# Fourteen products of the identity on TensorE behind the last turn of a decoder's front

## The reference, cut to what matters

```
h = rmsnorm(x, lp['ln_mix_g'])      # x (tokens, 2048)
proj = h @ lp['w_in']               # w_in (2048, 4352)
```

## Time and profile before

| what | us |
| --- | --- |
| runs of the kernel before, median | 2083.53 |
| the three runs | 2083.18, 2083.53, 2086.49 |
| the profiled execution | 2078.16 |
| its span, first to last instruction | 2076.5 |
| end of TensorE's last turn in `load_front` | 30.07 |
| first product of `project_in` | 36.12 |

### The profile page before, as it was taken

One profiled execution on the slowest core, in us unless ns is written; L12 is line 12 of the kernel. 1 busy time (PEld: TensorE's weight loads), 2 busy tenths in 40 slices (PEclk: granted clock), 3 DMA queues, 4 the chain that ended last, 5 costly groups with the idle time before them and its releaser, 6 DMA issues. The chain is left out here.

```text
span 2076.5 us, 38289 instructions
## 1 busy us (share of the span) xinstructions
PE 1879.5 (91%) x15850; PEld 1277.5 (62%) x15850; DVE 706.3 (34%) x1361; ACT 511.4 (25%) x866; POOL 140.1 (7%) x180
## 2 busy tenths in 40 slices
PE   6999996788989989989878999999999999999993
PEld 6999985675665549978544555444554444455441
DVE  4447767425545544355441111111111111111111
ACT  4446532232213222263241101110111011101111
POOL 0000000400132300000000000000000000000000
PEclk9999996788999999999988999999999999999997
DMA  8545521113133429443869999999999999999996
GB/s 227 143 124 140 142 74 23 24 39 101 62 112 111 136 78 287 120 142 94 318 253 375 423 422 424 423 426 395 410 422 425 422 423 401 412 424 422 422 424 223
DMA packets 210765, 543.62 MB, mean 262 GB/s; under 512 B 44536, under 2 KB 168538, under 8 KB 183632
## 3 DMA queue, kind: packets, MB, share of 16 engines
q1 hardware_dynamic: 202274, 532.97, 67.3%
q0 software_dynamic: 7936, 8.68, 2.0%
q10 hardware_dynamic: 438, 0.32, 0.1%
HBM read 524.86 MB, written 28.59 MB: 267 GB/s over the span
## 5 line engine op out<-in xcount | busy, mean ns | idle before, releaser
L2848 PE MATMUL p_u<-w_expert,xgT 128*64 128x256 f32 x2048 | 239.6, 388 | 34.0 <-DMA w_expert<-in_w_up_dram 34.0
L2848 PE MATMUL p_g<-w_expert,xgT 128*64 128x256 f32 x2048 | 231.9, 379 | 0.9 <-DVE xgT L2928 0.9
L2848 PEld LDWEIGHTS p_u<-w_expert,xgT 128*64 128x64 f32 x2048 | 148.6, 140 | 117.6 <-DMA w_expert<-in_w_up_dram 43.1
L2864 PE MATMUL p_y<-w_expert,hidT 128*64 128x512 f32 x960 | 217.8, 595 | 0.8 <-DVE hidT L2940 0.5
L2848 PEld LDWEIGHTS p_g<-w_expert,xgT 128*64 128x64 f32 x2048 | 147.1, 137 | 88.0 <-issue 18.8
L2816 PE MATMUL p_xg<-low,slot_sel 128*64 128x512 f32 x768 | 179.7, 604 | 5.2 <-DVE slot_sel L2912 5.2
L2864 PEld LDWEIGHTS p_y<-w_expert,hidT 128*64 128x64 f32 x960 | 66.2, 137 | 126.0 <-issue 124.1
L2933 DVE CAST row<-rowf 128x1 int32<-128x1 f32 x32 | 4.9, 154 | 357.6 <-POOLq L3023 357.6
L2983 ACT ACTIVATE act_g<-p_g 128x256 f32<-128x256 f32 x32 | 12.3, 384 | 429.2 <-PE p_u L2848 429.2
L3020 POOL DMA_INDIRECT x_dram<-y_slots,row x32 | 49.9, 1559 | 973.2 <-DVE y_slots L2944 973.2
L2816 PEld LDWEIGHTS p_xg<-low,slot_sel 128*64 128x64 f32 x768 | 52.9, 138 | 86.0 <-issue 75.6
(11 more groups left out here) (571 smaller groups left out, 2614.4 us busy)
## 6 DMA issues: line engine op xcount, KB each, us to landing
w_expert<-in_w_gate_dram SPq DMA_DIRECT2D x64, 2048.0 KB, 22.6
w_expert<-in_w_up_dram SPq DMA_DIRECT2D x64, 2048.0 KB, 24.7
w_expert<-in_w_down_dram SPq DMA_DIRECT2D x60, 2048.0 KB, 20.3
w_in_raw<-in_w_in_dram SPq DMA_DIRECT2D x32, 1024.0 KB, 5.6
lat<-in_cache_kv_latent_dram SPq DMA_DIRECT2D x128, 128.0 KB, 2.1
ho_raw<-in_w_out_dram SPq DMA_DIRECT2D x12, 1024.0 KB, 6.7
tables_sb<-in_w_out_dram SPq DMA_DIRECT2D x4, 1024.0 KB, 8.3
mem_k_s<-in_cache_mem_k_dram SPq DMA_DIRECT2D x8, 512.0 KB, 6.6
```

The source lines that it names most:

```text
L2848: mm = pe.matmul(acc[SL * h:SL * h + SL, 0:FF // 2], xgT[:, t, g // 2, :], w[g][:, FF * t + FF // 2 * h:FF * t + FF // 2 * h + FF // 2], s ...
L2864: mm = pe.matmul(p_y[SL * h:SL * h + SL, 512 * b:512 * b + 512], hidT[:, j, g, :], tile, start=(g == 0 and j == 0), stop=(g == 1 and j == 1))
```

## The change

Behind the last turn, TensorE waits until ScalarE has made its ninth copy, that of bank `p_r[0]` for the third token tile, and then multiplies the identity by the identity fourteen times into the first 128 columns of that bank. Each is a product of its own (it starts and stops its sum). Nobody reads the result.

```
                 turn_raw(2)
                 turn_scaled(1)
                 turn_scaled(2)
+                pe.wait_ge(raw_copied, 9)
+                for _ in range(14):
+                    pe.matmul(p_r[0][:, 0:128], S.ident, S.ident, start=True, stop=True)
```

## The result

| | median, us | runs |
| --- | --- | --- |
| before | 2083.67 | 22, from 2077.05 to 2090.59 |
| changed | 2089.55 | 22, from 2084.91 to 2095.24 |

The ratio is 1.0025, with a 95% interval of 1.0016 to 1.0035: the change makes the kernel slower by 5.9 us, where no change (2083.6, range 2080.5 to 2087) was forecast.

What follows compares the result with a forecast made beforehand. TensorE was busy 91% of the span, with front shifts carried on. Barrier +0.7 us, partly offset by a warmer clock, left -0.1 to +0.4 us; +0.1 on the 2083.53 median gave 2083.6 us, range 2080.5 to 2087.

Steps and rivals of the forecast that it cites:

- What bounds the kernel, and the meeting of the blocks: Front's end: barrier opens 0.28 us after VectorE, the last to arrive; a front shift reaches the end one for one at best.
- The wait on `raw_copied`: Behind TensorE's last turn: the count reaches 9 at 25.39 us, TensorE comes at 30 us, so it costs nothing.
- The products' price: Ahead of the barrier: 28 passes, 0.118 us each at full clock (3.3 us) or 0.213 at half (6.0 us).
- Which clock they get: Products ahead of the barrier: 16 passes at half clock, then 12 at full, ending at 35.0; barrier +0.7 us.
- rival B: Products ahead of the barrier: half clock throughout, barrier 1.85 us late, third tile +1.1 us, 2084.6 us; chance 0.12.
- The third tile: Projection: the DMA, issued later behind the barrier, moves the cast's end to 52.0; tile starts at 52.05, not 52.15.
- What comes back: Projection's start: full clock ends two tiles at 50.9, leaving the third 0.1 us earlier; 0.35 late if the clock falls.
- The penalty by the Trainium skill: Half-clock stretch 30.07 to 40.3 us: throttled time x (1 - K/N), an estimated 5.1 us; the rows give less, 2.0 us.
- rival C: Half-clock stretch at the front: gain by the skill's penalty, or a luckier clock later, -5.1 us or more, 2078.4; chance 0.04.
- Rival D: Later stages: the shift adds half-clock stretches under dense products, 1.7 us each, three for +5 us, 2088.6; chance 0.06.

Runs made afterwards that it cites:

- the 8 us barrier: Kernel before, no products, GpSimd clearing a spent buffer twenty times ahead of the barrier; first cast 7.6 us late, kernel 7.0 us slower by the medians, ratio 1.0035.
- b4_change_again: The change with its fourteen products once more, against the kernel before; ratio 1.0021 (1.0008 to 1.0034).
- b1_shift_undone: The change plus 200 empty TensorE instructions in projection tiles 6 to 30, 256 with the change's 56, against the kernel before; ratio 1.0013 (1.0000 to 1.0025).

## Why the prediction was wrong, point by point

**What bounds the kernel, and the meeting of the blocks**: right. The barrier waits for TensorE, opens 0.26 to 0.28 us behind TensorE or VectorE as the last engine (0.48 behind GpSimd's last clear, 36.64 to 37.12), and the front's shift reaches the end one for one within the interval, as the 8 us barrier shows.

**The wait on `raw_copied`**: right, nothing.

**The products' price**: right. 28 passes, 0.213 us at the half clock, 0.118 at the full one; 6.01 us in the first profile of the change, 5.02 in the second.

**Which clock they get**: the forecast (half, then full from some 3.4 us on) is what the two profiles of `b4_change_again` and `b1_shift_undone` show; rival B (half throughout) is, but for three passes, what the first profile of the changed kernel shows, where the clock fell at 28.6, ahead of the products, and stayed low for 6.8 us. Counted from the last turn's start, 4.98 us ahead of the cast before, the barrier was 1.9 us late in it (36.19 - 29.30) and 0.7 in `b4_change_again` (35.81 - 30.14); +0.7 was forecast. So the term was right in its likelier form, and the chance of B was set low at 0.12: one of three.

**The third tile**: wrong, and this is the first step that failed. I let its cast's end move by as much as the barrier, 52.0, as the DMA is issued by so much later. The DMA also took longer: from issue to cast 11.6 us before, and 13.3, 13.0 and 14.3 in the three profiles with fourteen products. In all others, with seven, with one column, with empty instructions or with a late barrier alone, it is 11.5 to 12.3. The first of the DMA's sixteen parts lands 14.1 to 14.3 us behind the barrier in every profile; it is the last that comes late. The term is 1.4 to 2.7 us, where I had 0. What holds up that last part is open, but the traces have a lead. TensorE's next packet of instructions starts 13.1 to 14.6 us behind the barrier in all six kernels with products ahead of the projection, beside this DMA's end, and 17.1 to 17.6 behind it, when all parts have landed, in the other eleven. None of the eleven is late; of the six the three with fourteen products are, and those with one column or seven are not, so the packet alone doesn't do it.

**What comes back**: wrong in sign. I counted the full clock's gain at the projection's start as 0.1 us left at the third tile, after its cast. It is worse than lost: TensorE arrives there early and waits 2.4 and 3.7 us, the clock falls, and the third tile runs at the half clock. Its sixteen first products took 4.01 and 4.63 us for 2.61. With the later cast this makes the fourth tile start 2.7 (first profile), 3.6 and 5.5 us late, where -0.1 to +0.4 was forecast for the third and was to be carried on. The view for it was at hand: the earlier trace rows shows the clock falling behind an idle stretch, and I had worked out a wait at the third tile without asking what the clock does there. A late barrier of 2.5 us without products, which is a little more than the change's own, costs a ratio of 1.0013 and 1.0014, some 3 us; the change with the shift undone 1.0013.

**What the prediction did not have at all**: that 56 instructions on TensorE's queue can cost something 290 us later. Kernels with 56 more instructions and an untouched front gave 1.0025, 1.0010 and 1.0007, on average 1.0014, 2.9 us; with 256, 128 and 200 they gave 1.0004, 0.9998 and 1.0004, with 28 1.0015, and the same program again 1.0012. The average of the first three lies above that of the other three by 0.12%, which is half the width of one interval. That the grid of dry places moves is shown, to the instruction, and so is one price of its move, the 0.6 to 1.3 us at the output projection; that the whole costs time at 56, and not at 128, 200 and 256, is what the runs point to, and the size, 2 to 3 us, is uncertain by about as much as it is. The late front (3 us) and the moved grid (2 to 3 us) together make the 5.9 us of the change, and the seven products without either make 1.0002. That a late front is carried to the end I hold for shown; that it is 3 us of the change rests on three ratios (1.0013, 1.0014, 1.0013) whose intervals begin at 0.9999 to 1.0001. The second I hold for likely.

**The penalty by the Trainium skill** ("TensorE: Matmul & The Clock Gate", section Terms): the estimate of 5.1 us, read as a gain in rival C, came to nothing. The trace does not agree with the rule read so: the clock was full from 34.4 to 54.9 in `b4_change_again`, and the kernel was slower.

**Rival D** (a late knock-on, from the clock, +5 us) had the right sign and nearly the size, and 0.06; its mechanism was another. The range ended at 2087, 3.4 us above the likeliest time, made up of the runs' spread; it did not take in a DMA that lands late (1.4 to 2.7 us here), nor a clock that falls at the third tile (1.4 and 2.0 us on its first sixteen products).

## What to carry to other kernels

Filler work ahead of a barrier has to end before the engine that arrives last, at the slower clock; here seven products fitted and fourteen did not. Warming the clock bought nothing here, where the next thing that the engine met was a wait for a DMA: it got to the wait earlier, stood longer, and the clock fell there. And a change's instructions count, not only their time: with passes of 12 ns the queue ran dry at fixed counts, the packets that fill it held up a DMA beside them, and a few instructions more at the front moved both through all that follows; compare with the same number of empty instructions, and with as many as fill the grid's distance, before a result of 0.1 or 0.2% is put down to the change itself.

## What the runs showed of the hardware

In streams of short passes TensorE's queue ran dry at each 256th of its instructions, for 1.4 to 2.4 us each time in L942 (idle time of its loads), about 3.7 us from one start to the next (411.43, 415.39, 418.86, 422.54), and went on 1.2 to 1.6 us behind the end of a 16 KB packet of instructions. In 8 of 8 profiles in which such a packet fell beside the DMA of `xT_again`, the last of that DMA's parts landed 9.8 to 10.4 us behind its issue; in the other 9 it was 9.2 to 9.3. Where products take 0.147 us there is no stop at these places. 200 and 256 empty instructions in the projection's dense stretch cost no time that the runs can tell (1.0004 both).

One program's executions spread over 13 us (2077.05 to 2090.59), and ratios over 12 and 35 of them missed 1 by 0.12% with an interval that left it out; effects of 0.1% need more than one such comparison.
